# Page loads of the paged attention divided by tensor instead of by batch, with four value slots instead of eight

## The chip, the cores and the metric

The kernel runs on one core of a Trainium2 chip. The metric is the device time of one launch in microseconds. Before the change it is 3706.94 us, the median of three runs (3704.8 to 3708.46).

## The reference

One inference step of a two-layer decoder, for a prompt of 1024 tokens and for 8 sample sequences of 8 new tokens each, with the same weights. Layer 0 runs gated linear attention beside a sparse attention (DSA), layer 1 a window attention; a SwiGLU block follows each. The part that matters here is the sparse attention of the sample sequences. It picks 256 of 2056 keys for each new token with an indexer, and attends to these:

```
def dsa_sample(layer, q, k_new, v_new, iq, ik_new, iw, cache_k, cache_v, cache_idx, page_table):
    ...
    _, idx = lax.top_k(sc, kk)
    ...
    phys = page_table[bidx, ip // PAGE_SIZE]
    ...
    ks = jnp.where(in_past, cache_k[layer, phys, off], k_new[bidx, inew])
    vs = jnp.where(in_past, cache_v[layer, phys, off], v_new[bidx, inew])
    return dsa_attend(q, ks, vs, idx <= t[None, :, None])
```

Keys and values of the 2048 past tokens of a sequence lie in 16 pages of 128 tokens, which a page table names. A page of keys is 128 tokens by 2 heads by 64 numbers, 64 KB, and a page of values as much. The kernel loads every page and masks what was not picked.

## The kernel before

The program is a row of stages with a barrier of all engines between them. `even_in` projects layer 0 and runs the indexer of the samples; `dsa_sample` (lines 1565 to 1870) is the stage of this change, from about 600 to 820 us; `dsa_out` finishes the prompt's sparse attention; the two-part SwiGLU, layer 1 and its SwiGLU follow. No engine works ahead over a stage's end, apart from one thing that `dsa_sample` does for the next stage (below).

`dsa_sample` holds 8 sequences ("batches" b = 0 to 7) in 4 pairs (p = 0 to 3). For each pair TensorE transposes the 32 pages of keys (`keys_T`, L1696), ScalarE copies them to `KT` (L1619), TensorE makes the scores (L1715 adds the mask by a product of `spb` and `bias`, L1718 is query times key), VectorE takes the row maximum (L1857), ScalarE the exponential (L1788), TensorE transposes the probabilities (L1732) and multiplies them with the 32 pages of values (L1744, `Vp`), and VectorE scales the result into `yq` (L1869), which GpSimd stores (L1655).

VectorE and TensorE also do work for the next stage here: the indexer scores of two blocks of the prompt. TensorE makes 32 products of queries and index keys (L1683, 64 instructions in the trace), ScalarE applies the relu to them (L1774), VectorE adds them with weights (L1827 for a first head, L1830 for the rest, `add_dot`), and then searches the 256 largest of each row in rounds of eight (L1839 and L1840, `search_round`, 32 rounds for each block). Ten rounds stand ahead of the first pair, the rest are spread over the four pairs. VectorE's program begins with two short steps: a memset, and L1814, which makes the bf16 tile `spb` out of a constant (`spread`) that comes by DMA into `spf`, a view of the tile `PT`. Its wait is `dve.wait_ge(cin, 32)`, and everything that VectorE does in the stage stands behind it.

Two queues load the pages, that of SyncE (SP) and that of GpSimd (POOL). Both call `load_pages`: a loop on the issuing engine, whose turn reads four entries of the page table into registers (L58) and then issues the loads of these four pages (L63), here a key page and a value page each. SP takes batches 0, 2, 4, 6 and GpSimd 1, 3, 5, 7. Keys have four slots (`Kp`), so a load of batch 4 and up waits for the transposes of batch b - 4 (`kt_done`); values have eight slots (`Vp`), one for each batch, and wait for nothing. On SP the small loads stand ahead of all pages: page table, index keys (`KI`), index queries (`IQ`), causal mask, spread, bias. The new values (`Vn`, L1643) stand behind batch 0. The order is written out by hand.

Of the kernel before, what the change touches and what calls it, by code (L numbers as in the profile page):

```python
# [15 lines left out]
P = 128  # L16
D = 1024
KD = D // P
SEQ, DEC_BATCH, DEC_SEQ = 1024, 8, 8
# [22 lines left out]
PAGES = 16  # L42
# [12 lines left out]

def load_pages(eng, pages, n_pool, b, j0, j1, places, group=4):
    with eng.Fori(j0 // group, j1 // group) as g:
        at = [eng.value_load(pages[0:1, bass.ds(g * group + (b * PAGES + r), 1)], min_val=0, max_val=n_pool - 1) for r in range(group)]  # L58
        for r in range(group):
            for cache, dst_of, landed in places:  # L60
                src = cache[bass.ds(at[r], 1)]
                src = src.rearrange("o p k d -> (o p) (k d)") if len(src.shape) == 4 else src.rearrange("o p d -> (o p) d")
                eng.dma_start(dst_of(bass.ds(g * group + r, 1)), src).then_inc(landed, 16)  # L63

# [39 lines left out]
def even_in(nc, st, A, C, O, x_tile, H, Hs):  # L104
# [35 lines left out]
    with ExitStack() as ctx:  # L140
# [127 lines left out]
        with ExitStack() as early, nc.Block() as block:  # L268
# [27 lines left out]
            def index_slot(p):  # L296
                return (idxb[:, 0], idxb[:, 1], staged_keys, idxb[:, 0])[p]

            def load_index(eng, b, j0, j1, group=4):
                dst_of = lambda j: index_slot(b // 2)[:, j, b % 2, :].rearrange("p o d -> p (o d)")  # L300
                load_pages(eng, pages, n_pool, b, j0, j1, [(A["cache_idx"][0], dst_of, ix_in[b])], group)

# [1262 lines left out]
def dsa_sample(nc, st, A, C, O, Hs, XT, bias_ahead):  # L1565
# [7 lines left out]
    with ExitStack() as ctx:  # L1573
# [12 lines left out]

        Vp, Vn = sb("Vp", [P, NB, PAGES, P]), sb("Vn", [DEC_SEQ, NB, P])
        Pb, PT = sb("P", [P, LK]), sb("PT", [P, PAGES + 1, P])
# [5 lines left out]
        cin, pin = sem("const_in"), sem("page_table_in")  # L1594
        k_in, v_in = [sem(f"k_pages{k}") for k in range(4)], [sem(f"v_pages{b}") for b in range(NB)]
        bias_in, vn_in = sem("bias_in"), sem("v_new_in")
# [23 lines left out]

        def load(eng, b):
            if b >= 4:
                eng.wait_ge(kt_done, 4 * (b - 3))
            key_of = lambda j: Kp[:, b % 4, j, :].rearrange("p o c -> p (o c)")
            value_of = lambda j: Vp[:, b, j, :].rearrange("p o c -> p (o c)")
            load_pages(eng, pages, n_pool, b, 0, PAGES, [(A["cache_k"][0], key_of, k_in[b % 4]), (A["cache_v"][0], value_of, v_in[b])])

        with nc.Block() as block:
            @block.sync
            def _(sp):  # L1630
                sp.dma_start(pages[:, :], A["page_table"].rearrange("(o a) b -> o (a b)", o=1)).then_inc(pin, 16)
                sp.dma_start(KI[:, :, :], st.h_dram[:, C_IK - W0:C_IK - W0 + W_KI].rearrange("(t p) c -> p t c", p=P)).then_inc(ki_in, 16)
                for a in range(AHEAD):
                    t = BLOCK[2 + a]
                    sp.dma_start(IQ[:, a, :], st.h_dram[t * P:(t + 1) * P, C_IQ - W0:C_END - W0]).then_inc(ki_in, 16)
                sp.dma_start(causal[:, :], C["causal"]).then_inc(mask_in, 16)
                for f in range(2):
                    sp.dma_start(spf[NS * f:NS * f + NS, :, :], C["spread"]).then_inc(cin, 16)
                sp.dma_start(bias[:, :], st.bias_dram).then_inc(bias_in, 16)
                sp.wait_ge(pin, 16)  # L1640
                load(sp, 0)
                for b in range(NB):
                    sp.dma_start(Vn[:, b, :], Hs[8 * b:8 * b + 8, C_DV:C_DV + P]).then_inc(vn_in, 16)  # L1643
                for b in (2, 4, 6):
                    load(sp, b)

            @block.gpsimd
            def _(pool):
                pool.wait_ge(pin, 16)
                for b in (1, 3, 5, 7):  # L1650
                    load(pool, b)
                for p in range(NP_):
                    pool.wait_ge(y_done, p + 1)
                    for b2 in range(2):
                        pool.dma_start(bass.AP(scr_y.tensor, (2 * p + b2) * DEC_SEQ * 512, [[HD, 8], [512, DEC_SEQ], [1, HD]]),  # L1655
                                       yq[64 * b2:64 * b2 + 64, p, :]).then_inc(y_out, 16)
                pool.wait_ge(y_out, 32 * NP_)
                pool.dma_start(Hs[0:NS, C_DQ:C_DQ + 512], scr_y).then_inc(y_in, 16)
                pool.wait_ge(y_in, 16)

            @block.tensor
            def _(pe):
# [42 lines left out]
                for p in range(NP_):  # L1705
# [33 lines left out]
                    for b2 in range(2):  # L1739
                        vs = 2 * p + b2  # L1740
                        pe.wait_ge(v_in[vs], 16 * PAGES)
                        r = slice(64 * b2, 64 * b2 + 64)
                        for j in range(PAGES):
                            nc.tensor.matmul(ps[r, 7, 0:P], PT[:, j, r], Vp[:, vs, j, :], start=(j == 0), stop=False)  # L1744
                        last = nc.tensor.matmul(ps[r, 7, 0:P], PT[0:DEC_SEQ, PAGES, r], Vn[:, 2 * p + b2, :], start=False, stop=True)
# [1451 lines left out]
```

## Time and profile before

| | |
|---|---|
| median of 3 runs | 3706.94 us |
| profiled execution, its own time | 3706.94 us |
| its span | 3705.2 us |
| TensorE busy over the span | 89% |
| VectorE busy over the span | 43% |
| the stage of the change, 600 to 828 us | 6% of the span |
| VectorE busy from 613.8 to 812 us | 189.16 of 198.2 us |
| TensorE busy there | 121.25 us |

The page's shares are means over stages. Over the whole span TensorE is the busiest engine, but in the stage of the change it is not. A stage is to be read by itself: its windows, the timeline of the engine that is never idle there, and what that engine waited for before it began.

### The profile page before, as it was taken

What the parts mean: (1) busy time and instruction counts of PE and PEld (TensorE: products, weight loads), DVE (VectorE), ACT (ScalarE), POOL (GpSimd) and SP (SyncE); (2) the same over time, 40 slices, a digit from 0 to 9 for tenths busy, and PEclk for the clock granted to TensorE, in tenths of its full rate; (3) what the DMA queues carried; (4) which work ended last, traced back from release to release, by engine and by line L of the source; (5) the groups of instructions that cost most, each with busy time, mean ns of one, the idle gap of its engine ahead of it and who ended that gap; (6) DMA issues with size and microseconds to landing.
All of it is one profiled execution on the core that took longest, in us unless ns stands there. A gap on an engine that the chain in (4) does not pass through costs nothing. (4 is left out here: it accounts for less than half of the span.)

```text
span 3705.2 us, 52838 instructions
## 1 busy us (share of the span) xinstructions
PE 3297.7 (89%) x20520; PEld 2822.8 (76%) x20539; DVE 1604.1 (43%) x2853; ACT 1088.9 (29%) x2145; POOL 357.6 (10%) x472
## 2 busy tenths in 40 slices
PE   7998887637888988999998996987998999999997
PEld 7797764424445547999998996974665999999997
DVE  2186764974677322111114564323544111112566
ACT  2223543214233332111113443122443111112443
POOL 1100113402111000000000001530000000000002
PEclk9998885867888688999999998987998999999999
DMA  4211004403000001111103111212001111112111
GB/s 128 60 35 31 27 25 136 126 18 122 18 18 23 12 12 57 40 45 45 45 28 106 44 49 52 46 59 87 32 29 46 44 42 45 45 40 97 39 57 49
DMA packets 234467, 190.84 MB, mean 52 GB/s; under 512 B 53762, under 2 KB 211860, under 8 KB 234260
## 3 DMA queue, kind: packets, MB, share of 16 engines
q1 hardware_dynamic: 225540, 168.63, 14.9%
q0 software_dynamic: 8752, 19.81, 1.7%
q8 instruction: 118, 1.93, 0.2%
q14 instruction: 57, 0.47, 0.0%
HBM read 158.73 MB, written 31.38 MB: 51 GB/s over the span
## 5 line engine op out<-in xcount | busy, mean ns | idle before, releaser
L1973 PE MATMUL ffn1u_ps<-h_hi,ffn1u_whi 128*128 128x384 f32 (+1 forms) x1056 | 348.7, 330 | 8.8 <-DVE h_lo L2035 8.8
L1973 PE MATMUL ffn0u_ps<-h_hi,ffn0u_whi 128*128 128x384 f32 (+1 forms) x1056 | 345.2, 327 | 8.6 <-DVE h_lo L2035 8.6
L1973 PE MATMUL ffn1u_ps<-h_hi,ffn1u_wlo 128*128 128x384 f32 (+1 forms) x1056 | 348.5, 330 | 0.0
L1973 PE MATMUL ffn1u_ps<-h_lo,ffn1u_whi 128*128 128x384 f32 (+1 forms) x1056 | 348.5, 330 | 0.0
L1973 PE MATMUL ffn0u_ps<-h_hi,ffn0u_wlo 128*128 128x384 f32 (+1 forms) x1056 | 345.4, 327 | 0.0
L1973 PE MATMUL ffn0u_ps<-h_lo,ffn0u_whi 128*128 128x384 f32 (+1 forms) x1056 | 345.1, 327 | 0.0
L198 PE MATMUL ine_ps<-ine_w_hi,ine_x_hi 128*128 128x256 f32 (+2 forms) x864 | 263.7, 305 | 6.8 <-DVE ine_w_lo L214 5.1
L198 PE MATMUL ine_ps<-ine_w_hi,ine_x_lo 128*128 128x256 f32 (+2 forms) x864 | 249.2, 288 | 0.0
L198 PE MATMUL ine_ps<-ine_w_lo,ine_x_hi 128*128 128x256 f32 (+2 forms) x864 | 248.4, 288 | 0.0
L1973 PEld LDWEIGHTS ffn1u_ps<-h_hi,ffn1u_whi 128*128 128x128 f32 x1056 | 199.4, 189 | 9.1 <-DVE ffn1u_wlo L2017 9.1
L1973 PEld LDWEIGHTS ffn0u_ps<-h_hi,ffn0u_whi 128*128 128x128 f32 x1056 | 198.8, 188 | 9.0 <-DVE ffn0u_wlo L2017 9.0
L1973 PEld LDWEIGHTS ffn1u_ps<-h_lo,ffn1u_whi 128*128 128x128 f32 x1056 | 199.4, 189 | 0.0
L1973 PEld LDWEIGHTS ffn1u_ps<-h_hi,ffn1u_wlo 128*128 128x128 f32 x1056 | 199.3, 189 | 0.0
L1973 PEld LDWEIGHTS ffn0u_ps<-h_lo,ffn0u_whi 128*128 128x128 f32 x1056 | 198.8, 188 | 0.0
L1973 PEld LDWEIGHTS ffn0u_ps<-h_hi,ffn0u_wlo 128*128 128x128 f32 x1056 | 198.7, 188 | 0.0
L2121 PE MATMUL ffn0d_ps<-ffn0d_w_hi,ffn0d_a_hi 128*128 128x256 f32 (+1 forms) x594 | 171.2, 288 | 13.2 <-DVE ffn0d_X L2223 6.5
L2121 PE MATMUL ffn1d_ps<-ffn1d_w_hi,ffn1d_a_hi 128*128 128x256 f32 (+1 forms) x594 | 171.2, 288 | 13.0 <-DVE ffn1d_X L2223 6.5
L198 PEld LDWEIGHTS ine_ps<-ine_w_hi,ine_x_hi 128*128 128x128 f32 (+1 forms) x864 | 165.9, 192 | 20.0 <-issue 8.5
L2121 PE MATMUL ffn0d_ps<-ffn0d_w_hi,ffn0d_a_lo 128*128 128x256 f32 (+1 forms) x594 | 170.2, 287 | 0.0
L2121 PE MATMUL ffn0d_ps<-ffn0d_w_lo,ffn0d_a_hi 128*128 128x256 f32 (+1 forms) x594 | 170.1, 286 | 0.0
L2121 PE MATMUL ffn1d_ps<-ffn1d_w_hi,ffn1d_a_lo 128*128 128x256 f32 (+1 forms) x594 | 169.8, 286 | 0.0
L2121 PE MATMUL ffn1d_ps<-ffn1d_w_lo,ffn1d_a_hi 128*128 128x256 f32 (+1 forms) x594 | 169.6, 286 | 0.0
(465 smaller groups left out, 7340.0 us busy)
## 6 DMA issues: line engine op xcount, KB each, us to landing
ffn0u_raw<-in_ffn_w_gu_dram SPq DMA_DIRECT2D x44, 512.0 KB, 3.7
ffn1u_raw<-in_ffn_w_gu_dram SPq DMA_DIRECT2D x44, 512.0 KB, 3.7
ffn0d_w<-in_ffn_w_down_dram SPq DMA_DIRECT2D x88, 128.0 KB, 2.1
ffn1d_w<-in_ffn_w_down_dram SPq DMA_DIRECT2D x88, 128.0 KB, 2.1
ine_w<-in_w_in_even_dram SPq DMA_DIRECT2D x5, 1024.0 KB
scratch_h<-ine_stage SPq DMA_DIRECT2D x20, 256.0 KB, 2.5
idx_keys<-in_x_prompt_dram SPq DMA_DIRECT2D x8, 512.0 KB, 3.9
idx_w<-in_w_in_even_dram SPq DMA_DIRECT2D x4, 1024.0 KB, 5.4
```

What stands on the lines that cost most here:

```text
L198: last = nc.tensor.matmul(o, xp[:, k, i * P:i * P + r], wp[:, g % RING, 0:n], start=(k == 0 and j == 0 and i % 2 == 0), stop=(k == KD - 1 ...
L1973: last = nc.tensor.matmul(ps[:, t, k2, 0:n], wp[:, k2, k, :], hp[:, k, t0:t0 + n], start=(k == 0 and j == 0), stop=(k == KD - 1 and j == 2))
L2121: last = nc.tensor.matmul(acc(i), ap[:, n % 2, i * P:i * P + rows(i)], wp[:, k, :], start=(k == 0 and j == 0 and i % 2 == 0), stop=(k == K ...
```

## The change

`load_pages` loads pages of one cache in a call, not of two. In `dsa_sample` the tile `Vp` has four slots, as `Kp` has. SP now loads the keys of all eight batches, and the values of batches 6 and 7 behind them, which wait until the second pair is done (`y_done` at 2). GpSimd loads the values of batches 0 to 3 at once, and those of batches 4 and 5 between its two stores of the first pair's result. The key loads of batches 0 and 1 stand ahead of the loads of spread and bias on SP. TensorE waits on the semaphores of the new slots. The indexer stage calls `load_pages` in its new form with the same loads as before.

```
-def load_pages(eng, pages, n_pool, b, j0, j1, places, group=4):
+def load_pages(eng, pages, n_pool, b, j0, j1, cache, dst_of, landed, group=4):
     with eng.Fori(j0 // group, j1 // group) as g:
         at = [eng.value_load(...) for r in range(group)]
         for r in range(group):
-            for cache, dst_of, landed in places:
-                src = cache[bass.ds(at[r], 1)]
...
-                eng.dma_start(dst_of(bass.ds(g * group + r, 1)), src).then_inc(landed, 16)
+            src = cache[bass.ds(at[r], 1)]
...
+            eng.dma_start(dst_of(bass.ds(g * group + r, 1)), src).then_inc(landed, 16)
...
-        Vp, Vn = sb("Vp", [P, NB, PAGES, P]), sb("Vn", [DEC_SEQ, NB, P])
+        Vp, Vn = sb("Vp", [P, 4, PAGES, P]), sb("Vn", [DEC_SEQ, NB, P])
...
-        def load(eng, b):
-            if b >= 4:
-                eng.wait_ge(kt_done, 4 * (b - 3))
...
-            load_pages(eng, pages, n_pool, b, 0, PAGES, [(A["cache_k"][0], key_of, k_in[b % 4]), (A["cache_v"][0], value_of, v_in[b])])
+        def load(eng, b, cache, dst, slot, landed):
+            load_pages(eng, pages, n_pool, b, 0, PAGES, cache, lambda j: dst[:, slot, j, :].rearrange("p o c -> p (o c)"), landed)
...
                 sp.dma_start(causal[:, :], C["causal"]).then_inc(mask_in, 16)
+                sp.wait_ge(pin, 16)
+                load(sp, 0, A["cache_k"][0], Kp, 0, k_in[0])
+                load(sp, 1, A["cache_k"][0], Kp, 1, k_in[1])
                 for f in range(2):
                     sp.dma_start(spf[NS * f:NS * f + NS, :, :], C["spread"]).then_inc(cin, 16)
                 sp.dma_start(bias[:, :], st.bias_dram).then_inc(bias_in, 16)
-                sp.wait_ge(pin, 16)
-                load(sp, 0)
                 for b in range(NB):
                     sp.dma_start(Vn[:, b, :], Hs[8 * b:8 * b + 8, C_DV:C_DV + P]).then_inc(vn_in, 16)
-                for b in (2, 4, 6):
-                    load(sp, b)
+                for b in range(2, NB):
+                    if b >= 4:
+                        sp.wait_ge(kt_done, 4 * (b - 3))
+                    load(sp, b, A["cache_k"][0], Kp, b % 4, k_in[b % 4])
+                sp.wait_ge(y_done, NP_ - 2)
+                for b in range(NB - 2, NB):
+                    load(sp, b, A["cache_v"][0], Vp, b % 4, v_last_in[b % 2])
...
                 pool.wait_ge(pin, 16)
-                for b in (1, 3, 5, 7):
-                    load(pool, b)
+                for b in range(4):
+                    load(pool, b, A["cache_v"][0], Vp, b % 4, v_in[b % 4])
                 for p in range(NP_):
                     pool.wait_ge(y_done, p + 1)
                     for b2 in range(2):
                         pool.dma_start(bass.AP(scr_y.tensor, ...), yq[64 * b2:64 * b2 + 64, p, :]).then_inc(y_out, 16)
+                        if p + 3 < NP_:
+                            load(pool, 2 * p + 4 + b2, A["cache_v"][0], Vp, (2 * p + b2) % 4, v_in[(2 * p + b2) % 4])
...
-                        vs = 2 * p + b2
-                        pe.wait_ge(v_in[vs], 16 * PAGES)
+                        vs = (2 * p + b2) % 4
+                        if p < NP_ - 1:
+                            pe.wait_ge(v_in[vs], 16 * PAGES * (p // 2 + 1))
+                        else:
+                            pe.wait_ge(v_last_in[b2], 16 * PAGES)
```

The first place is the SP queue behind its first small loads. Before, this stands in a row there, ahead of every page (`smp_PT` is the tile that holds the spread constant, `smp_pages` the page table in SBUF):

```order
172 L1631 DMA smp_pages<-in_page_table_dram 1x128
173 L1632 DMA smp_KI<-scratch_h 128x8x136
174 L1635 DMA smp_IQ<-scratch_h 128x512 x2
175 L1636 DMA smp_causal<-const_causal 128x128
176 L1638 DMA smp_PT<-const_spread 64x512 x2
177 L1639 DMA smp_bias<-scratch_bias 128x1032
```

With the change the spread and the bias stand behind two loops of key loads, of four turns each; this is the end of the second loop and what follows:

```order
211 L62 ISA
212 L62 REGISTER_ALU
213 L62 DMA smp_Kp<-in_cache_k_dram 128x128
214 L62 ISA
215 L62 REGISTER_ALU
216 L62 DMA smp_Kp<-in_cache_k_dram 128x128
217 L57 REGISTER_ALU
218 L57 COMPARE_AND_BRANCH
219 L1637 DMA smp_PT<-const_spread 64x512 x2
220 L1638 DMA smp_bias<-scratch_bias 128x1032
221 L1640 DMA smp_Vn<-Hs 8x128 x8
```

So 32 page loads, and the register work of eight turns, have moved ahead of the two loads of the spread constant.

The second place is the end of a turn of SP's first page loop. Before, two loads follow from one entry of the page table:

```order
200 L63 ISA
201 L63 DMA smp_Kp<-in_cache_k_dram 128x128
202 L63 REGISTER_ALU
203 L63 DMA smp_Vp<-in_cache_v_dram 128x128
204 L57 REGISTER_ALU
205 L57 COMPARE_AND_BRANCH
```

and now one does, in a loop that still reads four entries for each turn:

```order
190 L62 ISA
191 L62 DMA smp_Kp<-in_cache_k_dram 128x128
192 L62 ISA
193 L62 DMA smp_Kp<-in_cache_k_dram 128x128
194 L57 REGISTER_ALU
195 L57 COMPARE_AND_BRANCH
```

The same entry is now read once for the keys and once more for the values: the program has 64 such turns in this stage where it had 32, 40 of them on SP (16 before) and 24 on GpSimd (16 before).

## Rows read from the trace of the kernel before

**Rows 1.** Windows of the stage: length, busy time by engine, TensorE's granted clock, DMA share, GB/s.
```profile
core 0: us, PE busy (x) PEld busy (x) DVE busy (x) ACT busy (x) POOL busy (x), PEclk, DMA share, GB/s
...
600.00:613.80 13.80, 7.19 (x29) 5.11 (x30) 1.23 (x4) 3.78 (x8) 4.67 (x9) 0.50 0.66 197
613.80:812.00 198.20, 121.25 (x628) 74.86 (x624) 189.16 (x253) 53.44 (x99) 67.66 (x126) 0.78 0.28 81
812.00:828.00 16.00, 1.11 (x8) 0.92 (x8) 0.88 (x4) 0.58 (x1) 1.66 (x3) 0.50 0.03 10
```

**Rows 2.** Timeline of VectorE at the stage's start: start, duration, instruction, [idle before].
```profile
607.84 0.43 DVE L1814 CAST smp_spb<-smp_PT 128x512 bf16<-128x512 f32 x1 [6.38 <-DMA smp_PT<-const_spread]
...
613.84 0.49 DVE L1827 TENSOR_SCALAR smp_sc<-smp_rel,smp_iws 128x512 f32<-128x512 f32 x1 [5.22 <-ACT smp_rel L1774]
615.47 0.48 DVE L1827 TENSOR_SCALAR smp_sc<-smp_rel,smp_iws 128x512 f32<-128x512 f32 x1 [1.14 <-ACT smp_rel L1774]
616.06 11.87 DVE L1830 SCALAR_TENSOR_TENSOR smp_sc<-smp_rel,smp_iws,smp_sc 128x512 f32<-128x512 f32 x14
627.96 0.29 DVE L1837 TENSOR_TENSOR smp_sc<-smp_sc,smp_causal 128x128 f32<-128x128 f32 x1
```

**Rows 3.** Waits of VectorE from 600 to 828 us: us in total, times, longest.
```profile
DVE smp_spb L1814 <- DMA smp_PT<-const_spread: 6.4, 1, 6.4
DVE smp_sc L1827 <- ACT smp_rel L1774: 6.4, 2, 5.2
...
DVE smp_mx L1857 <- PE smp_ps L1718: 0.6, 1, 0.6
```

**Rows 4.** Timeline of all engines at the stage's end.
```profile
811.76 1.17 DVE L1869 TENSOR_SCALAR smp_yq<-smp_ps,smp_rs 32x64 f32<-32x64 f32 x4
813.22 1.11 POOL L1655 DMA_DIRECT2D scratch_y<-smp_yq  x2 [31.14 <-DVE smp_yq L1869]
```

**Rows 5.** Timeline of SyncE in the stage.
```profile
603.13 1.18 SPq L1638 DMA_DIRECT2D smp_PT<-const_spread  x2
604.36 0.59 SPq L1639 DMA_DIRECT2D smp_bias<-scratch_bias  x1
608.09 0.37 SPq L63 DMA_DIRECT2D smp_Kp<-in_cache_k_dram  x1
...
635.44 5.53 SPq L1643 DMA_DIRECT2D smp_Vn<-Hs  x8
644.28 0.35 SPq L63 DMA_DIRECT2D smp_Kp<-in_cache_k_dram  x1
```

**Rows 6.** Timeline of SyncE in the indexer stage: index pages, one load for each entry.
```profile
36.31 42.86 SPq L63 DMA_DIRECT2D idx_keys<-in_cache_idx_dram  x32
...
42.72 2.26 SPq L63 DMA_DIRECT2D idx_keys<-in_cache_idx_dram  x4
...
48.10 2.26 SPq L63 DMA_DIRECT2D idx_keys<-in_cache_idx_dram  x4
```

**Rows 7.** DMA issues of SyncE: KB each, median us from issue to landing.
```profile
smp_Kp<-in_cache_k_dram SPq DMA_DIRECT2D x64, 64.0 KB, 2.0
...
smp_PT<-const_spread SPq DMA_DIRECT2D x2, 128.0 KB, 4.1
```

**Rows 8.** Timeline of GpSimd in the stage.
```profile
605.44 0.61 POOL L63 DMA_DIRECT2D smp_Kp<-in_cache_k_dram  x1 [33.49 <-issue]
...
610.02 0.54 POOL L63 DMA_DIRECT2D smp_Vp<-in_cache_v_dram  x1
613.49 0.54 POOL L63 DMA_DIRECT2D smp_Kp<-in_cache_k_dram  x1 [2.93 <-issue]
...
744.75 1.11 POOL L1655 DMA_DIRECT2D scratch_y<-smp_yq  x2 [11.18 <-DVE smp_yq L1869]
```

**Rows 9.** Timeline of TensorE: first key transposes, values of pairs 2 and 3.
```profile
652.15 6.42 PE L1696 MATMUL smp_ps<-ident,smp_Kp 128*128 128x128 f32 x32 [5.20 <-ACT smp_rel L1774]
...
759.25 3.71 PE L1744 MATMUL smp_ps<-smp_Vp,smp_PT 128*64 128x128 f32 x32 [0.36 <-ACT smp_PT L1804]
...
793.96 3.71 PE L1744 MATMUL smp_ps<-smp_Vp,smp_PT 128*64 128x128 f32 x32
```

More of the change, by code:

```diff
@@ L59, in load_pages @@
         for r in range(group):
-            for cache, dst_of, landed in places:
-                src = cache[bass.ds(at[r], 1)]
-                src = src.rearrange("o p k d -> (o p) (k d)") if len(src.shape) == 4 else src.rearrange("o p d -> (o p) d")
-                eng.dma_start(dst_of(bass.ds(g * group + r, 1)), src).then_inc(landed, 16)
+            src = cache[bass.ds(at[r], 1)]
+            src = src.rearrange("o p k d -> (o p) (k d)") if len(src.shape) == 4 else src.rearrange("o p d -> (o p) d")
+            eng.dma_start(dst_of(bass.ds(g * group + r, 1)), src).then_inc(landed, 16)
 def bcast_rows(ap1d, n, parts=P):
@@ L299, in load_index @@
             def load_index(eng, b, j0, j1, group=4):
-                dst_of = lambda j: index_slot(b // 2)[:, j, b % 2, :].rearrange("p o d -> p (o d)")
-                load_pages(eng, pages, n_pool, b, j0, j1, [(A["cache_idx"][0], dst_of, ix_in[b])], group)
+                load_pages(eng, pages, n_pool, b, j0, j1, A["cache_idx"][0],
+                           lambda j: index_slot(b // 2)[:, j, b % 2, :].rearrange("p o d -> p (o d)"), ix_in[b], group)
             def wait_staged(eng):
@@ L1594, in dsa_sample @@
         cin, pin = sem("const_in"), sem("page_table_in")
-        k_in, v_in = [sem(f"k_pages{k}") for k in range(4)], [sem(f"v_pages{b}") for b in range(NB)]
+        k_in, v_in = [sem(f"k_pages{k}") for k in range(4)], [sem(f"v_pages{k}") for k in range(4)]
+        v_last_in = [sem("v_last_pages0"), sem("v_last_pages1")]
         bias_in, vn_in = sem("bias_in"), sem("v_new_in")
@@ L1619, in copy_keys @@
             op(KT[:, g // 4 % 2, 512 * (g % 4):512 * (g % 4 + 1)], ps[:, 5 + g % 2, :]).then_inc(key_copy(g)[0], 1)
-        def load(eng, b):
-            if b >= 4:
-                eng.wait_ge(kt_done, 4 * (b - 3))
-            key_of = lambda j: Kp[:, b % 4, j, :].rearrange("p o c -> p (o c)")
-            value_of = lambda j: Vp[:, b, j, :].rearrange("p o c -> p (o c)")
-            load_pages(eng, pages, n_pool, b, 0, PAGES, [(A["cache_k"][0], key_of, k_in[b % 4]), (A["cache_v"][0], value_of, v_in[b])])
+        def load(eng, b, cache, dst, slot, landed):
+            load_pages(eng, pages, n_pool, b, 0, PAGES, cache, lambda j: dst[:, slot, j, :].rearrange("p o c -> p (o c)"), landed)
         with nc.Block() as block:
```

## The prediction

> **What bounds the kernel now.** The change touches one stage, so I looked for the engine that sets that stage's length. The windows of the stage come first: from 613.8 to 812 us VectorE is busy 189.16 of 198.2 us, TensorE 121.25 and ScalarE 53.44 [rows 1]. VectorE's list of waits comes next. In the whole stage it waited 6.4 us for the spread constant, 6.4 us for the first two relu results, and only 0.6 us after that [rows 3]. No wait for a key page or a value page is among them: such waits fall on TensorE, which has room. The third view is the end. VectorE's last step starts at 811.76, GpSimd stores its result at 813.22, and after 828 the next stage runs [rows 1, 4]. So from its first weighted add at 613.84 [rows 2] to the end, the stage is one unbroken row of VectorE work, and its length is the time at which that row begins plus about 198 us. Page loads can only matter in two ways: they delay the start of VectorE's row, or they come so late that VectorE waits in it.
>
> **The first part: the spread constant behind 32 key loads.** VectorE's row begins with the cast L1814, which waited for the spread constant and ran at 607.84 [rows 2]. SP issued the two loads of the constant from 603.13 on, ahead of all pages [rows 5]. Now 32 key loads in eight turns stand ahead of it. VectorE keeps its program order, and everything in the stage stands behind L1814.
>
> When does SP get there? In the old order the first page load comes 3.14 us after the end of the load before it (604.36 + 0.59 = 604.95, then 608.09) [rows 5]. The loops now start where the spread stood, 603.13, so the first key load is issued at 603.13 + 3.14 = 606.27.
>
> How long are 32 single loads in eight turns? The stage itself has no such loop, but the indexer stage has the same helper with one load for each entry on the same engine: 32 loads in 42.86 us [rows 6]. Two neighbouring turns there start 5.38 us apart (42.72 to 48.10), and the four loads of a turn take 2.26 us, so eight turns without a disturbance are 7 x 5.38 + 2.26 = 39.9 us [rows 6]. These are my two ends; they lie close, and I take the middle, 41.4. The last key load is then over at 647.7.
>
> The second load of the constant is issued 0.6 us later (half of 1.18 us for two [rows 5]), 648.3. Its landing took 4.1 us before, beside traffic of 197 GB/s; a key load of half its size lands in 2.0 us [rows 1, 7]. These are again two ends, and I take 3.0: the same transfer with less beside it (the mean later in the stage is 81 GB/s [rows 1]). The cast then starts at 651.3. The cast and two small steps behind it took 0.8 us (607.84 to 613.84 less the 5.22 us of idle time [rows 2]), so the first weighted add starts at 652.1 instead of 613.84.
>
> A little comes back. TensorE and ScalarE don't wait for the spread constant, so four relu results lie ready, and the 1.14 us of idle time before the second add [rows 2] is gone. From the first add to L1837 it was 14.12 us (613.84 to 627.96), and it will be 12.98. L1837 starts at 652.1 + 12.98 = 665.1 instead of 627.96: VectorE's row is 37.2 us late. TensorE's and ScalarE's later steps move with it, since their own chains hang on the adds (the relu buffers are four deep) and then on each pair's maximum.
>
> With the low ends (39.9 and 2.0) it is 34.6 us, with the high ends (42.86 and 4.1) 39.7 us.
>
> A rule of the Trainium skill speaks against this term. Its page "DMA: Bandwidth & Descriptors", section "Issuing engines are not separate DMA queues", says that spreading DMAs over several issuing engines saves only the sequencer's time to initiate them, "which is usually small relative to the DMA itself". By that rule the order on SP would hardly matter, and what it would give is the first rival below. The trace disagrees for these loads: a turn of four loads costs SP 5.38 us, while each of them lands 2.0 us after its issue [rows 6, 7].
>
> **The second part: the key loads of pairs 1 to 3.** Before, two engines issued keys; now SP alone. Behind the spread come the bias and the eight loads of new values, 1.8 + 5.53 us, and 3.3 us of loop entry (640.97 to 644.28) [rows 5]. Batch 2 starts at 647.7 + 0.1 + 1.8 + 5.6 + 3.3 = 658.5. A pair of batches takes 41.4 us plus 3.1 us of entry, 44.5 in all: batches 2 and 3 are issued by 700, 4 and 5 by 744, 6 and 7 by 789. TensorE's first key transposes were at 652.15 [rows 9] and the first two batches are in by 650, long before the moved 689. For the rest, TensorE needs a pair when the moved scores of the pair before are done: about 702, 734 to 750 and 771 to 790. The waits for `kt_done` are over by then. Here some waits of one to five microseconds on TensorE are possible in the last pair. They cost nothing, because VectorE wants scores some 8 us after they are made (VectorE waited for scores 0.6 us in all [rows 3]). Cost: 0, and at most 5 us.
>
> **The third part: the values.** GpSimd's turn of eight loads took 8.05 us (605.44 to 613.49), and 3.47 of these from the start of the last load to the next turn (610.02 to 613.49) [rows 8]. Four loads at about 0.7 us apart make a turn of 5.6 us, so batches 0 to 3 are in by 605.4 + 16 x 5.6 = 695 us, ahead of every moved use. Batches 4 and 5 wait for the first pair's result on VectorE, at about 742 with the shift, and take two times 22.4 us: they are in by 790. Their use was at 759.25 [rows 9], moved 796. Cover 6 us. The stores of `yq` that now stand behind these loads are read by nobody before the end of the stage.
>
> Batches 6 and 7 are the tail of SP. The second pair's result was stored at 744.75 [rows 8], moved 782, so SP does not wait: it ends batch 7 of the keys at 789 and then issues 32 value loads, 3.1 + 41.4 us, until 833.5, landed at 835.5. TensorE multiplies with batch 7 for 3.71 us (it was at 793.96 [rows 9]) and is done at 840. VectorE's last step, at 811.76 before [rows 4], wants that at 849. Cover 9 us, cost 0. This is the thinnest cover of the change.
>
> **The sum.** +37.2 us for the late start, 0 for the rest. Fewer value slots and the loops' extra register work lie on queues, not on VectorE. GpSimd's stores at the end are as before. The profiled execution took 3706.94 us, of which the span is 3705.2; it is also the median of the runs, so the sum needs no correction: 3706.9 + 37.2 = 3744.1, rounded to 3744.
>
> **The rivals.**
> - *Transfer time, not issue time, delays the constant* (the rule above). The 32 key pages are 2.1 MB; at the 197 GB/s of the stage's start [rows 1] they take 10.6 us. The cast moves from 607.84 to 618.4 then, the first add to 619.2, 5.4 us late, and 1.1 us of that comes back: +4.3 us, 3711. That is no loss that can be told from no change, and the case on the other side. Against it stand 42.86 us for 32 loads of half the size [rows 6]. I give it 3 in 100. With it I count 2 in 100 that the stages behind gain more than this.
> - *SP's tail sets the end.* SP issues ten batches in five pairs. If a pair takes 48 us instead of 44.5 (a loop at 44.9 us in place of 41.4, 2 us slower than the slower of my two rows), the start is 3.5 us later and the tail 17.5 us, 14 more than the start, against a cover of 9: the end moves by 37.2 + 17.5 - 9 = 46 us, 3753. It decides from a pair of about 46.8 us on. For it speaks that two queues now load at once with more turns for each byte; against it that both queues already ran beside each other in the row of 42.86 us. 12 in 100.
> - *TensorE's clock.* The stage is at a granted clock of 0.78, with 0.50 before 613.8, the lower of its two levels, 1.2 GHz [rows 1]. TensorE now idles from its eighth product to 652. That costs nothing in this stage, with VectorE as its bound, but the next stages could come out a few microseconds off either way. This widens the range and has no case of its own.
>
> **How the numbers follow.** The likeliest case, the late start alone, has 83 in 100 and by itself 3740 to 3748. The tail has 12, the two small cases 5. The range takes in the first two: 3739 to 3753. A measurement of this kernel can tell about 0.2% (7.4 us) from no change. Both large cases are slower by far more, so slower has 0.95; within 0.2% has 0.03 by the first rival; faster has 0.02.
>
> **What would show it.** In the profile after: L1814 starts at 648 to 654 us with an idle time of some 46 to 53 us before it, ended by the spread constant's DMA. The list of waits names that for VectorE with about 50 us. The weighted adds start 35 to 40 us late, and the last step of VectorE in the stage is at about 849. VectorE's busy time in the stage is unchanged. The last value loads on SP are issued at about 833. The prediction is wrong if L1814 runs before 630, if VectorE shows a wait for TensorE's values at the end (then the tail), or if the stages behind 865 us differ from those behind 828 by more than a few microseconds.

## The result, and the profile after

The changed kernel takes 3744.78 us (median of 4 runs, 3742.02 to 3746.85), the kernel before 3707.38 us on the same occasion (4 runs). The ratio is 1.0101, 95% interval 1.0084 to 1.0119. The forecast was 3744 us, slower, with a range of 3739 to 3753.

VectorE's list of waits in the stage, from 600 to 868 us of the profiled execution (us in total, times, longest), answers to [rows 3]:

```profile
DVE smp_spb L1821 <- DMA smp_PT<-const_spread: 48.4, 1, 48.4
DVE smp_qz L1819 <- PEq L3088: 6.0, 1, 6.0
DVE smp_mx L1864 <- PE smp_ps L1722: 0.7, 1, 0.7
```

The wait for the spread constant has grown from 6.4 to 48.4 us, the wait for the first relu results is gone, and the wait for scores is as small as before. (L1819, the memset, is the first step behind the barrier; it waited as long in the kernel before.)

This is VectorE's start of the stage (start, duration, instruction, idle before), the answer to [rows 2]:

```profile
653.25 0.43 DVE L1821 CAST smp_spb<-smp_PT 128x512 bf16<-128x512 f32 x1 [48.40 <-DMA smp_PT<-const_spread]
653.59 0.46 DVE L1826 TENSOR_SCALAR smp_iws<-smp_KI 128x8 f32<-128x8 f32 x2
654.08 0.94 DVE L1834 TENSOR_SCALAR smp_sc<-smp_rel,smp_iws 128x512 f32<-128x512 f32 x2
655.12 11.87 DVE L1837 SCALAR_TENSOR_TENSOR smp_sc<-smp_rel,smp_iws,smp_sc 128x512 f32<-128x512 f32 x14
667.02 0.29 DVE L1844 TENSOR_TENSOR smp_sc<-smp_sc,smp_causal 128x128 f32<-128x128 f32 x1
```

And this is SyncE's row in the stage, the answer to [rows 5]:

```profile
604.19 0.30 SPq L1627 DMA_DIRECT2D smp_pages<-in_page_table_dram  x1
...
609.63 39.97 SPq L62 DMA_DIRECT2D smp_Kp<-in_cache_k_dram  x32
649.81 1.18 SPq L1637 DMA_DIRECT2D smp_PT<-const_spread  x2
651.03 0.58 SPq L1638 DMA_DIRECT2D smp_bias<-scratch_bias  x1
651.66 5.66 SPq L1640 DMA_DIRECT2D smp_Vn<-Hs  x8
660.61 126.17 SPq L62 DMA_DIRECT2D smp_Kp<-in_cache_k_dram  x96
790.27 42.47 SPq L62 DMA_DIRECT2D smp_Vp<-in_cache_v_dram  x32
867.59 0.35 SPq L1143 DMA_DIRECT2D dsa_causal<-const_causal  x1
```

In this execution the stage begins 3.4 us later than in the profile of before (604.19 against 600.79 for the page table's load), with the same code ahead of it, so starts are to be compared after taking off 3.4. The last row is the next stage's first load: the stage is 867.59 - 604.19 = 263.4 us long, against 827.96 - 600.79 = 227.2 before. That is +36.2 us. Nearly all of the change is in this stage: the time from there to the end is 2879.2 us, against 2877.2. The profiled execution took 3748.45 us and is not among the four of the median. The 3.4 us by which its stage begins later are part of that; over all the kernels below the stage begins between 598.7 and 605.3 us, so they are not put down to the change.

The windows answer to [rows 1]: VectorE has the same 189 us of work in a stretch of 198.5 us as before, and a hole ahead of it.

```profile
core 0: us, PE busy (x) PEld busy (x) DVE busy (x) ACT busy (x) POOL busy (x), PEclk, DMA share, GB/s
...
613.80:651.50 37.70, 5.21 (x17) 1.97 (x16) 0.00 (x0) 2.76 (x5) 14.98 (x28) 0.64 0.35 100
651.50:850.00 198.50, 117.41 (x616) 74.61 (x616) 188.82 (x253) 51.90 (x96) 37.79 (x70) 0.77 0.24 67
```

TensorE's own list of waits names no key page in this kernel. The thin cover of the forecast is at the end of the stage. These are TensorE's values of the last two batches, and VectorE's last step, the answers to [rows 9] and [rows 4]:

```profile
829.25 3.71 PE L1751 MATMUL smp_ps<-smp_Vp,smp_PT 128*64 128x128 f32 x32 [0.61 <-ACT smp_PT L1811]
...
834.18 3.71 PE L1751 MATMUL smp_ps<-smp_Vp,smp_PT 128*64 128x128 f32 x32 [0.86 <-DMA smp_Vp<-in_cache_v_dram]
```

```profile
851.04 1.17 DVE L1876 TENSOR_SCALAR smp_yq<-smp_ps,smp_rs 32x64 f32<-32x64 f32 x4
```

TensorE waits 0.86 us for the last value page and is done at 838.3; VectorE wants the result at 851.0. The cover is 12.8 us, so the tail of SyncE's queue did not set the end.

### The profile page after: what moved, and what is told of

It is laid out like the page before. It is cut to its first block and busy times, and to the rows that moved or that the text cites. A ratio compares the mean times of both kernels' runs of the same rounds, so it can differ in the third digit from the quotient of the medians.

```text
span 3746.8 us, 53513 instructions
## 1 busy us (share of the span) xinstructions
PE 3308.3 (88%) x20539; PEld 2829.9 (76%) x20539; DVE 1605.0 (43%) x2853; ACT 1089.8 (29%) x2145; POOL 340.2 (9%) x440
## 5 line engine op out<-in xcount | busy, mean ns | idle before, releaser
L197 PEld LDWEIGHTS ine_ps<-ine_w_hi,ine_x_lo 128*128 128x128 f32 (+1 forms) x864 | 167.9, 194 | 4.1 <-issue 4.1
```

Of the source, the lines that this page charges most:

```text
L197: last = nc.tensor.matmul(o, xp[:, k, i * P:i * P + r], wp[:, g % RING, 0:n], start=(k == 0 and j == 0 and i % 2 == 0), stop=(k == KD - 1 ...
```

## The experiments

Times are medians of 4 to 12 runs each, beside runs of the kernel before on the same chip (its medians there: 3709.39, 3709.55 and 3710.50 us). Behind the ratio stands its 95% interval. "Stage" is the time from the load of the page table to the next stage's first load in the profiled execution, "rest" from there to the end:

| kernel | time, us | ratio | stage, us | against 227.2 | rest, us |
|---|---|---|---|---|---|
| before | 3707.38 | | 227.2 | | 2877.2 |
| changed | 3744.78 | 1.0101 (1.0084, 1.0119) | 263.4 | +36.2 | 2879.2 |
| spread first | 3739.15 | 1.0080 (1.0066, 1.0094) | 253.8 | +26.6 | 2879.8 |
| spread behind batch 0 | 3738.49 | 1.0077 (1.0064, 1.0091) | 253.3 | +26.1 | 2873.2 |
| spread first, eight slots | 3734.90 | 1.0068 (1.0054, 1.0082) | 252.3 | +25.2 | 2876.7 |
| balanced | 3705.83 | 0.9990 (0.9981, 0.9999) | 223.3 | -3.9 | 2879.5 |
| before, spread late | 3733.81 | 1.0069 (1.0056, 1.0082) | 250.7 | +23.5 | 2879.3 |
| before, fewer search rounds | 3675.34 | 0.9907 (0.9893, 0.9921) | 195.2 | -32.0 | 2878.4 |
| changed, fewer search rounds | 3728.76 | 1.0061 (1.0040, 1.0081) | 251.2 | +24.1 | 2877.9 |
| changed, fixed pages | 3719.70 | 1.0026 (1.0017, 1.0035) | 236.4 | +9.3 | 2881.4 |
| balanced again | 3705.68 | 0.9989 (0.9981, 0.9998) | 223.6 | -3.6 | 2875.6 |
| balanced, scaling on ScalarE | 3699.02 | 0.9972 (0.9961, 0.9982) | 222.0 | -5.2 | 2870.3 |
| before, scaling on ScalarE | 3701.37 | 0.9982 (0.9970, 0.9995) | 222.5 | -4.6 | 2869.8 |

### The late start by itself

One edit to the kernel before, whose queues and eight slots stay as they are:

```
+                sp.wait_ge(pin, 16)
+                load(sp, 0)
                 for f in range(2):
                     sp.dma_start(spf[NS * f:NS * f + NS, :, :], C["spread"]).then_inc(cin, 16)
                 sp.dma_start(bias[:, :], st.bias_dram).then_inc(bias_in, 16)
-                sp.wait_ge(pin, 16)
-                load(sp, 0)
```

> The kernel before with its own queues and eight value slots, and one edit: spread and bias stand behind the loads of batch 0 (four turns of eight loads, 27 us) instead of ahead. Theory B and theory A agree here: nothing else is late, so the start alone counts. The cast runs at about 636 us instead of 608, VectorE's first search step is 22 us late, and all of it is seen at the end: 3727 to 3731 us. If the order on the queue did not matter (only the transferred bytes do), 3707 to 3712.

Measured: 3733.81 us, stage +23.5 us. Two waits of VectorE in it:

```profile
638.35 0.43 DVE L1814 CAST smp_spb<-smp_PT 128x512 bf16<-128x512 f32 x1 [36.28 <-DMA smp_PT<-const_spread]
...
689.23 2.30 DVE L1857 TENSOR_REDUCE smp_mx<-smp_ps 128x1 f32<-128x2056 f32 x1 [0.62 <-PE smp_ps L1718]
```

The time is 3 us over the expected band; the stage shows 23.5 us where 22 were expected. The cast comes 29.9 us later in its stage than before; 6.4 us of that come back, since the two waits for relu results in [rows 3] are gone. The first search step (652.07 in a stage that began at 601.41) is 23.5 us later, and the stage is longer by as much, in a kernel in which nothing else was touched.

### What the late start hides

The changed kernel, with the three small loads back in front:

```
                 sp.dma_start(causal[:, :], C["causal"]).then_inc(mask_in, 16)
+                for f in range(2):
+                    sp.dma_start(spf[NS * f:NS * f + NS, :, :], C["spread"]).then_inc(cin, 16)
+                sp.dma_start(bias[:, :], st.bias_dram).then_inc(bias_in, 16)
                 sp.wait_ge(pin, 16)
                 load(sp, 0, A["cache_k"][0], Kp, 0, k_in[0])
                 load(sp, 1, A["cache_k"][0], Kp, 1, k_in[1])
-                for f in range(2):
-                    sp.dma_start(spf[NS * f:NS * f + NS, :, :], C["spread"]).then_inc(cin, 16)
-                sp.dma_start(bias[:, :], st.bias_dram).then_inc(bias_in, 16)
```

> The changed kernel, with the loads of spread and bias put back ahead of the key loads of batches 0 and 1. Theory A (the late start is the whole cost, the new queues cost nothing): the stage is as before, ratio 1.000 to 1.002, about 3707 us. Theory B (the stage ends when the later of two rows ends, VectorE's and SyncE's; the late start of 36 us hides a second cost): SyncE now issues 10 batches at about 21.6 us each, so batch 3's keys land at about 699, batch 5's at 742, batch 7's at 785 on the clock of before. With TensorE's chain behind each pair (transposes, probabilities, values, scores: about 22 us) VectorE waits for the second, third and fourth scores and its row ends 24 to 29 us late: about 3734 us, ratio 1.0065 to 1.008. VectorE's waits then name TensorE's scores and values with 20 us or more.

Measured: 3739.15 us, stage +26.6 us. Theory A falls; the stage is in the middle of theory B's band of 24 to 29 us, though the time is 5 us above its 3734. The start is right again, and yet three quarters of the loss remain. VectorE's waits in the timeline of this kernel (every one behind the start of its row), and its last step:

```profile
665.82 2.30 DVE L1864 TENSOR_REDUCE smp_mx<-smp_ps 128x1 f32<-128x2056 f32 x1 [0.62 <-PE smp_ps L1722]
717.51 1.16 DVE L1876 TENSOR_SCALAR smp_yq<-smp_ps,smp_rs 32x64 f32<-32x64 f32 x4 [12.97 <-PE smp_ps L1752]
723.09 2.30 DVE L1864 TENSOR_REDUCE smp_mx<-smp_ps 128x1 f32<-128x2056 f32 x1 [4.41 <-PE smp_ps L1722]
763.50 2.30 DVE L1864 TENSOR_REDUCE smp_mx<-smp_ps 128x1 f32<-128x2056 f32 x1 [1.03 <-PE smp_ps L1722]
801.78 1.16 DVE L1876 TENSOR_SCALAR smp_yq<-smp_ps,smp_rs 32x64 f32<-32x64 f32 x4 [3.28 <-PE smp_ps L1752]
807.35 2.30 DVE L1864 TENSOR_REDUCE smp_mx<-smp_ps 128x1 f32<-128x2056 f32 x1 [4.41 <-PE smp_ps L1722]
...
838.41 1.16 DVE L1876 TENSOR_SCALAR smp_yq<-smp_ps,smp_rs 32x64 f32<-32x64 f32 x4
```

These are 26.7 us in six waits (the first, of 0.62, is there in the kernel before too), and the list of waits says where TensorE was: it waited for key pages, 55.3 us in all, where the kernel before has 12.6 us. The waits for values (L1752) have the same cause, because TensorE's program has the transposes of the next pair's keys ahead of this pair's values.

```profile
PE smp_ps L1700 <- DMA smp_Kp<-in_cache_k_dram: 55.3, 4, 17.6
```

SyncE's queue says which of its loads these are:

```profile
656.88 126.19 SPq L62 DMA_DIRECT2D smp_Kp<-in_cache_k_dram  x96
786.56 40.38 SPq L62 DMA_DIRECT2D smp_Vp<-in_cache_v_dram  x32
```

The last key load is issued at 783.07, 181.8 us into the stage. The fourth scores wait for it, and behind them VectorE works without a wait to its last step at 838.41. The eight turns of value loads behind the keys are not what ends this stage: TensorE waits 5.9 us for the last value page, but is done with it at 835.2, 3.2 us before VectorE asks.

A dose between the two: spread and bias between the key loads of batch 0 and batch 1.

```
                 sp.wait_ge(pin, 16)
                 load(sp, 0, A["cache_k"][0], Kp, 0, k_in[0])
-                load(sp, 1, A["cache_k"][0], Kp, 1, k_in[1])
                 for f in range(2):
                     sp.dma_start(spf[NS * f:NS * f + NS, :, :], C["spread"]).then_inc(cin, 16)
                 sp.dma_start(bias[:, :], st.bias_dram).then_inc(bias_in, 16)
+                load(sp, 1, A["cache_k"][0], Kp, 1, k_in[1])
```

> The changed kernel, with spread and bias between the key loads of batch 0 and batch 1: 16 loads ahead of them instead of 32. The cast should run at about 628 us on the clock of before (18.4 us of issue, then landing), so VectorE starts 14 us late. Theory A (late start alone): 3721 us. Theory B (the later of two rows): the same time as with spread first, about 3734 us, since SyncE's row is unchanged and is the later one with either start.

Measured: 3738.49 us, stage +26.1 us, the same as with spread first.

```profile
631.13 0.43 DVE L1821 CAST smp_spb<-smp_PT 128x512 bf16<-128x512 f32 x1 [25.79 <-DMA smp_PT<-const_spread]
...
682.07 2.30 DVE L1864 TENSOR_REDUCE smp_mx<-smp_ps 128x1 f32<-128x2056 f32 x1 [0.65 <-PE smp_ps L1722]
```

VectorE starts its row about 13 us late here (its first maximum is at 682.07 in a stage that began at 604.68, against 665.82 and 601.23 with spread first), and the end does not move. So the two costs are not added: the stage ends when the later of two rows ends. One is VectorE's own work, 198 us from its start; the other is SyncE's key loads, the fourth pair's scores, and what VectorE has to do behind these.

### Is it the reuse of slots?

Spread first, the same division over the queues, eight value slots, no load of values that waits for a result:

```
-        Vp, Vn = sb("Vp", [P, 4, PAGES, P]), sb("Vn", [DEC_SEQ, NB, P])
+        Vp, Vn = sb("Vp", [P, NB, PAGES, P]), sb("Vn", [DEC_SEQ, NB, P])
...
-                sp.wait_ge(y_done, NP_ - 2)
                 for b in range(NB - 2, NB):
-                    load(sp, b, A["cache_v"][0], Vp, b % 4, v_last_in[b % 2])
+                    load(sp, b, A["cache_v"][0], Vp, b, v_last_in[b % 2])
...
-                for b in range(4):
-                    load(pool, b, A["cache_v"][0], Vp, b % 4, v_in[b % 4])
+                for b in range(6):
+                    load(pool, b, A["cache_v"][0], Vp, b, v_in[b])
```

> As the kernel with spread first, with the same division of loads over the two queues, but with eight value slots and no load of values waiting for a result. Theory B (pace of SyncE's queue): the same as with spread first, about 3734 us. Theory C (reuse of four slots is what costs once the start is early): back to 3707 us, or clearly below the kernel with spread first.

Measured: 3734.90 us, stage +25.2 us. Theory C is excluded as the main cost; 1.4 us between the two stages is at the edge of what single profiles tell, and the intervals of the two ratios overlap. TensorE waits 54.9 us for key pages here too, so what costs is the pace of SyncE's queue, by the trace that of its key loads: one queue issues the keys of all eight batches.

The opposite edit keeps the four slots and divides both the keys and the values between the two queues, 32 turns on each:

```
+        def keys(eng, b):
+            if b >= 4:
+                eng.wait_ge(kt_done, 4 * (b - 3))
+            load(eng, b, A["cache_k"][0], Kp, b % 4, k_in[b % 4])
+
+        def values(eng, b):
+            if b >= 4:
+                eng.wait_ge(y_done, b // 2 - 1)
+            load(eng, b, A["cache_v"][0], Vp, b % 4, v_in[b % 4])
...
 (SyncE, behind spread, bias and the wait for the page table)
+                keys(sp, 0)
...
+                for what, b in ((values, 0), (keys, 2), (values, 2), (keys, 4), (keys, 6), (values, 4), (values, 6)):
+                    what(sp, b)
 (GpSimd, ahead of its stores)
+                for what, b in ((keys, 1), (values, 1), (keys, 3), (values, 3), (keys, 5), (keys, 7), (values, 5), (values, 7)):
+                    what(pool, b)
```

> Four value slots and one load for each entry as in the changed kernel, spread first, but 32 turns on each queue: SyncE loads keys and values of the even batches, GpSimd those of the odd ones, ordered by when they are needed. Theory B: each queue needs about 175 us, every pair is in before its use but for some 2 us at the third scores: 3706 to 3711 us, as before. Theory C (slot reuse costs) or a theory that reading the page table twice costs in itself: 3715 us or more.

Measured: 3705.83 us, stage -3.9 us. Four slots and one load for each table entry cost nothing when each queue carries half of the keys and half of the values. SyncE's last key load is now issued at 742.54, 139.2 us into the stage instead of 181.8:

```profile
702.27 40.27 SPq L62 DMA_DIRECT2D smp_Kp<-in_cache_k_dram  x32
```

This edit changes two things at once, the number of turns on a queue and the place of the keys. A kernel with 32 turns on each queue but all keys on SyncE's was not run. In the kernel with spread first the keys are SyncE's first 32 page turns already and come too late, so even numbers of turns alone should not mend it; that is read from the trace and not tested.

VectorE's waits in this stage are the ones of [rows 3]:

```profile
DVE smp_spb L1820 <- DMA smp_PT<-const_spread: 6.4, 1, 6.4
DVE smp_sc L1833 <- ACT smp_rel L1780: 6.3, 2, 5.2
...
DVE smp_mx L1863 <- PE smp_ps L1724: 0.6, 1, 0.6
```

That it is a little shorter than the kernel before was a surprise, so it was run again:

> The balanced kernel once more, for its distance to the kernel before. First theory: it is 3 to 4 us shorter, as its profile shows it, all of it between ScalarE's last copy in the stage and the next stage's first DMA (4.1 us where the kernel before has 8.0): ratio 0.999 again, with the same short gap. Second theory: the gap is chance of one execution, and the ratio is 1.000 within its interval.

Measured: 3705.68 us, ratio 0.9989 (0.9981, 0.9998), stage -3.6 us. The gap is short again. In the first run of this kernel:

```profile
821.97 0.59 ACT L1812 COPY YT_sample<-smp_ps 128x512 f32<-128x512 f32 x1 [29.48 <-PE smp_ps L1756]
826.61 0.35 SPq L1143 DMA_DIRECT2D dsa_causal<-const_causal  x1
```

From the end of the last copy to the next stage's first load it is 4.1 us, in both executions of this kernel; in the kernel before it is 827.96 - 819.97 = 8.0, in the changed one 8.3. It is 8.0 in every kernel here that is an edit of the kernel before (which divides its turns evenly too, 16 to each queue) and 8.3 in every edit of the changed one that keeps its division of the queues. What the engines do in it (the barrier, the clearing of semaphores) the profile does not show. It is repeatable; its cause stays open.

### Whose row ends the stage

Both kernels with 16 of the 32 search rounds of the second prompt block left out, which is work of VectorE alone:

```
-                rounds = [(a, k) for a in range(AHEAD) for k in range(ROUNDS)]
+                rounds = [(a, k) for a in range(AHEAD) for k in range(ROUNDS) if a == 0 or k < 15 or k == ROUNDS - 1]
```

> The kernel before, with 16 of the 32 search rounds of the second prompt block left out (that block's mask is then not the reference's). VectorE's row is 16 x 2.32 = 37 us shorter. If VectorE's row sets the stage, the whole is 33 to 37 us shorter, 3670 to 3674 us; if pages or TensorE's chain are close behind, less.

Measured: 3675.34 us, stage -32.0 us. Nearly all of the 37 us of work taken from VectorE is gained in the kernel before; the rest went into waits for scores (5.6 us in all, 3.1 at the fourth pair). TensorE's chain is the next limit, some 5 us behind; it waited 19.9 us for key pages itself, so the pages are part of that limit.

> The changed kernel, with the same 16 search rounds left out. Theory A (VectorE's row with its late start is all): 37 us shorter than the changed kernel, about 3708 us. Theory B: SyncE's tail sets the end, the last value page lands at 831 us on the clock of before, TensorE's last values end at 836 and the stage ends 24 us later than before, that is only 12 us earlier than in the changed kernel: about 3732 us, with VectorE waiting for TensorE's last values.

Measured: 3728.76 us, stage +24.1 us, which is 12.2 us less than the changed kernel's. Theory B had said +24 and 12, and 3732 us for the whole. VectorE now waits, at the end too:

```profile
799.75 1.17 DVE L1876 TENSOR_SCALAR smp_yq<-smp_ps,smp_rs 32x64 f32<-32x64 f32 x4 [10.95 <-PE smp_ps L1752]
805.32 2.30 DVE L1864 TENSOR_REDUCE smp_mx<-smp_ps 128x1 f32<-128x2056 f32 x1 [4.41 <-PE smp_ps L1722]
833.39 1.17 DVE L1876 TENSOR_SCALAR smp_yq<-smp_ps,smp_rs 32x64 f32<-32x64 f32 x4 [6.32 <-PE smp_ps L1752]
```

The last of these waits is for the last value page (TensorE waits 5.7 us for it), so here it is the eight turns of value loads at the end of SyncE's queue that end the stage.

### What 32 loads cost: bytes, issues or table reads

The changed kernel, with the first 32 key loads written out with page numbers that the program knows:

```
-                load(sp, 0, A["cache_k"][0], Kp, 0, k_in[0])
-                load(sp, 1, A["cache_k"][0], Kp, 1, k_in[1])
+                for b in range(2):
+                    for j in range(PAGES):
+                        sp.dma_start(Kp[:, b, j, :], A["cache_k"][0][PAGES * b + j].rearrange("p k d -> p (k d)")).then_inc(k_in[b], 16)
```

> The changed kernel with the 32 key loads ahead of spread as plain loads from fixed page numbers 0 to 31: the same bytes and as many DMA issues, but no entry of the page table is read for them (so these two batches use other pages than the reference). If the bytes set the delay, nothing changes: 3744 us. If SyncE's work sets it: 32 issues at about 0.65 us are 21 us instead of 43, the cast runs at about 628 us on the clock of before and the rest of SyncE's row is 22 us earlier too, so VectorE's row is again the later one and 14 us late: 3719 to 3724 us.

Measured: 3719.70 us, stage +9.3 us.

```profile
606.16 16.21 SPq L1636 DMA_DIRECT2D smp_Kp<-in_cache_k_dram  x32
622.41 1.17 SPq L1638 DMA_DIRECT2D smp_PT<-const_spread  x2
...
633.16 125.73 SPq L62 DMA_DIRECT2D smp_Kp<-in_cache_k_dram  x96
```

The same 2.1 MB now take 16.2 us instead of 40.0, 0.51 us a load. So of a turn's 5.4 us, some 2 are the four issues and more than 3 are the reading of four table entries and the arithmetic on registers. The expected 0.65 us a load was too much, so the stage lost 9.3 us and not 14. That bytes set the delay is excluded, and also by the two rows with a table: 32 loads of 32 KB took 42.86 us [rows 6], 32 of 64 KB took 39.97.

### Work taken off VectorE

The experiments say that the kernel before and the balanced one are set by VectorE's row. So the four scalings of each pair's result went to ScalarE:

```
 (ScalarE, behind the copies of the probabilities)
+                    act.wait_ge(rs_done, p + 1)
+                    act.wait_ge(o_done, p + 1)
...
+                            ins = nc.scalar.activation(yq[r, p, :], ps[r, 7, kv * HD:(kv + 1) * HD], ACT.Copy, scale=rs[r, 0:1])
+                    ins.then_inc(y_done, 1)
 (VectorE)
-                    link(nc.vector.reciprocal(rs[:, :], sm[:, :]))
-                    dve.wait_ge(o_done, p + 1)
...
+                    nc.vector.reciprocal(rs[:, :], sm[:, :]).then_inc(rs_done, 1)
```

> The kernel before, with the same move of the scalings to ScalarE. If VectorE's row sets the stage: 3.5 us shorter, ratio 0.999. If TensorE's wait for the result (it may not write its bank before) matters: no change.

Measured: 3701.37 us, stage -4.6 us. Of the 4.6 us, 1.3 lie ahead of the first scaling: the first search step is 25.9 us into the stage here and 27.2 in the kernel before, with 4.4 us of waits for relu results instead of 6.4. The other 3.3 fit the expected 3.5.

> The balanced kernel (four slots, 32 turns on each queue, spread first), and the four small scalings of each pair's result (L1869 before, 1.17 us a pair) moved from VectorE to ScalarE, which was busy 53 of 198 us. If VectorE's row sets the stage, it is three times 1.2 us shorter (the fourth pair's scaling is on the path on either engine): 3.5 us less than the balanced kernel, about 3702 to 3703 us. If something else is as late as VectorE, no change against the balanced kernel.

Measured: 3699.02 us, ratio 0.9972 (0.9961, 0.9982), stage -5.2 us. It is the shortest of all the kernels that leave no search rounds out, and shorter than the kernel before beyond its interval. Against the balanced kernel its stage gained only 1.5 us of the expected 3.5, since VectorE waits 2.8 us for scores there instead of 0.6; both kernels gained more in time than in their stage. What is left lies behind the stage: the rest is 2870 us against 2877. In the kernel before with this edit, 6.1 of these 7.4 us are gained ahead of the first load of the SwiGLU, which comes 586.6 us behind the stage's end instead of 592.7. This is a stretch ahead of it, from 372 to 572 us behind the stage's end, in the kernel before and in the kernel before with this edit:

```profile
1200.00:1400.00 200.00, 179.94 (x634) 104.15 (x639) 60.33 (x143) 60.61 (x125) 9.36 (x4) 0.75 0.04 14
```

```profile
1197.90:1397.90 200.00, 171.97 (x658) 98.09 (x664) 62.33 (x147) 62.47 (x129) 9.37 (x4) 0.84 0.04 15
```

TensorE's granted clock (the third figure from the end of a row) is a mean of 0.84 there instead of 0.75, a mix of the lower level, 1.2 GHz (0.50 in such rows), and the full 2.4 GHz (1.00), and it does 658 matmuls in the stretch instead of 634.

## Why the prediction was right, point by point

- *VectorE's row bounds the stage, and its start decides.* Shown three ways: VectorE's busy time and waits are the same behind the hole; the late spread alone costs 23.5 us of stage in the old kernel; 37 us less work on VectorE is 32 us less stage.
- *The issue of 32 key loads.* The first load was said to come at 606.27 and came at 609.63 - 3.4 = 606.2. The loop was put at 41.4 us between ends of 39.9 and 42.86, and took 39.97: the undisturbed pace of [rows 6] was the better of the two. The forecast is 1.4 us too long by this term.
- *The landing of the constant.* Taken as 3.0 us between 2.0 and 4.1; the two loads took 2.5 and 2.8.
- *The hand-over to the first add,* 0.8 us: 654.08 - 653.25 = 0.83. *What comes back,* 12.98 us to the first search step: 667.02 - 654.08 = 12.94.
- *The sum,* 37.2 us late: the first search step is at 667.02 - 3.4 = 663.6 against 627.96, 35.7 us late. The stage is 36.2 us longer. The 1.5 us between 37.2 and 35.7 are the loop's. That the median moved by 37.4 us, to within 1 us of the forecast, is in part luck: the four times spread over 4.8 us, and the profile shows 36.2 us in the stage and 2.0 behind it, for which the sum had no term.
- *The keys of the later pairs and the values cost 0.* Right as terms of this sum: the last batch's values had a cover of 12.8 us where 9 were named. But the text underrates what lies there. It priced the tail only at the end of the stage, and found it a thin cover of 9 us; it did not say what the new queues cost if the start were early, because it went through the keys with the start already late. That cost is 26.6 us, by the trace of the kernel with spread first the late keys of the later pairs, and 9.6 us under the late start it is the next limit. "0 for the rest" is true of the sum and false of the edit.
- *The rivals.* The transfer time rule (+4 us) is excluded by the fixed pages and by the late spread. The Trainium skill says, in "DMA: Bandwidth & Descriptors", section "Issuing engines are not separate DMA queues", that the time to initiate a DMA is usually small beside the DMA itself. The traces don't agree for these loads: each takes 1.25 us of SyncE in a loop with table reads and 2.0 us from issue to landing, and the landings overlap over many loads, while the issues don't. The tail did not set the end, but the experiment with fewer search rounds shows that it would have, 12 us earlier.

## What to carry to other kernels

Before you move a load past others on a queue, count the issuing engine's time for everything it is moved past, table reads included, and find out who stands behind the load's first reader: here a constant of 128 KB held up an engine that had 198 us of work behind it. When a loss has two causes that run beside each other, the time is that of the later one; undoing the larger one alone gives back only the difference (36 to 27 us here), so price each edit with the others undone. And divide over the queues the loads that are wanted soonest, not only the number of turns: with all keys on one queue the last key load was issued 43 us later than with half of the keys on each. When an engine's own row sets a stage, take work off that engine. The balanced kernel with its scaling moved is 0.3% shorter than the one before, with half of the value slots. Only 5.2 of its 11.5 us are in the stage, and 3.9 of these are the shorter gap at the stage's end. What shortened that gap and the time behind the stage is not shown.

## What the runs showed that was not expected

- The time behind the stage, in code that no kernel here touched, was 2869.8 to 2881.4 us over thirteen profiled executions. The three shortest (2869.8, 2870.3, 2873.2) are those in which TensorE's granted clock was 0.81 to 0.84 in the 200 us from 372 us behind the stage's end; in the rest it was 0.75 to 0.78. Why it was granted is not settled. The two kernels with the scaling on ScalarE had it in their profiles and are shorter by 9 and 11.5 us where their stages are shorter by 5, so it may well go with them; a reader should not put these microseconds down to VectorE's lighter row.
- The gap between the last copy of the stage and the next stage's first load is 4.1 us in each of the three profiles of the balanced kernel (its variant with the scaling on ScalarE among them) and 8.0 to 8.3 us in all others. It is the whole of what the balanced kernel gained, and what it hangs on is open: the kernel before divides its loads evenly too and has 8.0.
